# Score pairs of one map instead of two, and a value matmul in four parts, in a differential-attention encoder layer

## The reference

```python
s = jnp.einsum('bhqd,bhkd->bhqk', qblk, k, preferred_element_type=jnp.float32) * scale
p = jax.nn.softmax(s, axis=-1).reshape(B, N_HEADS, 2, Q_BLOCK, S)
a = p[:, :, 0] - lam * p[:, :, 1]  # differential attention map
return jnp.einsum('bhqk,bhkd->bhqd', a.astype(v.dtype), v)
```

## Time and profile before

| what | value |
|---|---|
| median of 3 runs (lowest, highest) | 4798.5 us (4790.17, 5101.57) |
| the profiled execution | 4784.27 us |
| its span on the slowest core | 4782.7 us (cores 4754.5 to 4782.7) |
| TensorE matmul busy | 4108.0 us (86%) |
| ScalarE busy | 2917.7 us (61%) |
| VectorE busy | 2577.9 us (54%) |
| GpSimd busy | 535.0 us (11%) |
| mean granted TensorE clock | 0.927 |
| moved by DMA | 752.94 MB, mean 157 GB/s |

### The profile page before, as it was taken

The page is one execution under the profiler, slowest core; times in us unless marked ns, Lnnn a source line. Parts: engine busy times, 40 slices in busy tenths (PEclk is TensorE's granted clock), DMA queues, the critical chain, the costliest instruction groups (busy, mean ns, idle before and its releaser), DMA issues.

```text
span 4782.7 us, 50532 instructions; the slowest of 8 cores (4754.5 to 4782.7 us)
## 1 busy us (share of the span) xinstructions
PE 4108.0 (86%) x18144; PEld 1551.1 (32%) x18144; DVE 2577.9 (54%) x4244; ACT 2917.7 (61%) x5274; POOL 535.0 (11%) x486
## 2 busy tenths in 40 slices
PE   6858666889898889896878898888899978999999
PEld 2312121223343333331223343323333323344344
DVE  2757545566434667675755425655677666323333
ACT  4658667778544668785877434567888866412411
POOL 1631010000001520000000003410000000000100
PEclk9978686999999999997989999999999989999999
DMA  9367796799895247779678752288777786524522
GB/s 231 82 156 154 168 190 135 166 187 195 182 253 169 82 124 155 141 165 200 130 162 204 196 142 73 68 201 206 174 158 167 150 206 153 183 84 154 187 87 80
DMA packets 1122593, 752.94 MB, mean 157 GB/s; under 512 B 917155, under 2 KB 1053606, under 8 KB 1097766
## 3 DMA queue, kind: packets, MB, share of 16 engines
q1 hardware_dynamic: 1044966, 507.47, 47.3%
q10 hardware_dynamic: 31968, 208.68, 13.4%
q0 software_dynamic: 45408, 33.56, 5.3%
HBM read 441.30 MB, written 115.34 MB: 116 GB/s over the span
## 4 chain that ended last, share of the span: by engine, by line
PE 46%; ACT 21%; DMA 15%; DVE 9%; issue 6%; POOL 2%; SPq 1%; ACTq 0%; DVEq 0%
PE pall L464 46%; ACT sb_ov L477 20%; DMA sb_ov<-sb_ov 13%; DVE sb_ov L488 5%; DVE sb_ov L485 3%; POOL sb_ov L485 2%; SPq L507 1%; ACT sb_sm L477 1%; DMA fr_d<-sb_ov 0%; DMA q_d<-sb_ov 0%; SPq L510 0%; DVE sb_sm L488 0%; DMA sb_ov<-x 0%; DVE sb_sm L797 0%; DMA sb_ov<-hT_d 0%
## 5 line engine op out<-in xcount | busy, mean ns | idle before, releaser
L464 PE MATMUL pall<-sb_ov 128*128 128x512 bf16 (+1 forms) x15588 | 3576.9, 392 | 521.2 <-ACT sb_ov L477 391.4
L477 ACT ACTIVATE sb_ov<-pall 128x1024 bf16<-128x1024 f32 (+2 forms) x2383 | 2036.9, 868 | 1207.4 <-PE pall L464 1002.0
L464 PEld LDWEIGHTS pall<-sb_ov 128*128 128x128 bf16 (+1 forms) x15588 | 1327.1, 98 | 2680.3 <-ACT sb_ov L477 723.2
L488 DVE SCALAR_TENSOR_TENSOR sb_ov<-sb_ov,sb_sm 128x2048 bf16<-128x2048 bf16 (+1 forms) x480 | 1026.3, 2138 | 255.4 <-ACT sb_sm L477 241.9
L485 DVE TENSOR_TENSOR sb_ov<-pall,sb_ov 128x512 f32<-128x512 f32 (+1 forms) x912 | 619.2, 690 | 600.4 <-PE pall L464 454.7
L485 POOL TENSOR_TENSOR sb_ov<-sb_ov 128x512 bf16<-128x512 f32 (+1 forms) x384 | 462.1, 1225 | 2334.9 <-DVE sb_ov L485 1837.7
L477 ACT ACTIVATE sb_ov<-sb_ov 128x512 f32<-128x512 f32 (+3 forms) x597 | 507.1, 850 | 239.6 <-DVE sb_ov L485 116.8
L485 DVE TENSOR_TENSOR sb_ov<-sb_ov 128x512 bf16<-128x512 bf16 (+2 forms) x530 | 348.1, 662 | 524.4 <-ACT sb_ov L477 465.2
L464 PE MATMUL pall<-sb_ov,sb_vall 128*128 128x512 bf16 x1536 | 398.8, 419 | 60.1 <-DMA sb_ov<-sb_ov 60.1
L477 ACT ACTIVATE sb_ov<-pall,sb_sm 128x512 f32<-128x512 f32 x384 | 262.5, 686 | 251.4 <-PE pall L464 115.0
L477 ACT ACTIVATION_READ_ACCUMULATOR sb_ov<-pall 128x1 f32 x1536 | 306.4, 199 | 0.0
(11 more groups left out here) (33 smaller groups left out, 223.9 us busy)
## 6 DMA issues: line engine op xcount, KB each, us to landing
sb_ov<-x SPq DMA_DIRECT2D x96, 512.0 KB, 8.0
sb_ov<-k_d SPq DMA_DIRECT2D x96, 512.0 KB, 4.8
sb_ov<-wb_g ACTq DMA_DIRECT2D x44, 1024.0 KB, 6.1
sb_ov<-wb_u ACTq DMA_DIRECT2D x40, 1024.0 KB, 5.6
sb_ov<-wb_d ACTq DMA_DIRECT2D x40, 1024.0 KB, 5.7
sb_ov<-wb_a ACTq DMA_DIRECT2D x44, 768.0 KB, 5.7
sb_ov<-hT_d SPq DMA_DIRECT2D x24, 1024.0 KB, 12.0
y<-sb_ov SPq DMA_DIRECT2D x48, 512.0 KB, 5.0
```

What stands on the lines that cost most here:

```text
L464: P.op("pe", lambda e: e.matmul(out, lhsT=lhsT, rhs=rhs, start=start, stop=stop), reads, writes, us)
L477: P.op("act", lambda e: e.activation(out=out, in_=in_, func=func, **kw), reads, writes, us)
L488: P.op(eng, lambda e: e.scalar_tensor_tensor(out=out, in0=in0, scalar=scalar, in1=in1, op0=op0, op1=op1), reads, writes, vus(eng, n) + 0.06)
```

## The change

A unit is now one map of one half: `sset(n, hh, m)` issues two score matmuls, key blocks 2hh and 2hh+1 of map m, one on rows 0 to 63 and one on rows 64 to 127, into the map's two banks, and one exponential. Before each unit stands a `Need` for its two banks alone. For that, k is stored with even key blocks on partitions 0 to 63 and odd ones on 64 to 127, both maps along the row, and q is stored twice, on both halves of the partitions. A q load is 256 KB into one of two buffers (three of 128 KB before); a q store is two DMAs. Buffers behind q move by 1 KB per partition. The value matmul yields an empty `Need` after 4, 8 and 12 of its 16 matmuls.

```diff
-    k_d = dscr("k_d", [8, 128, SEQ], BF16)
-    q_d = dscr("q_d", [8, 128, SEQ], BF16)
+    k_d = dscr("k_d", [8, 128, 2, 2, 512], BF16)
+    q_d = dscr("q_d", [8, 128, 2, SEQ], BF16)
...
-        A_T, A_K, A_Q, A_E1, A_E2, A_SQ, A_RS, A_D = 0, 32, 40, 43, 55, 63, 65, 69
+        A_T, A_K, A_Q, A_E1, A_E2, A_SQ, A_RS, A_D = 0, 32, 40, 44, 56, 64, 66, 70
...
-                    d, nm = (k_d, "k_d") if n < 32 else (q_d, "q_d")
-                    DMAL(d[hd % 8][:, c * 512:(c + 1) * 512], ovb(so, 512), ("st", n % 3), cells(so, 512), [(nm, hd % 8, c)], 128)
+                    if n < 32:
+                        dst = [(k_d[hd, 64 * (c % 2):64 * (c % 2) + 64, :, c // 2], ("k_d", hd, c))]
+                    else:
+                        dst = [(q_d[hd - 8, 64 * i:64 * i + 64, :, c * 512:(c + 1) * 512], ("q_d", hd - 8, c, i)) for i in range(2)]
+                    for i, (d, key) in enumerate(dst):
+                        DMAL(d.rearrange("d m t -> m d t"), ovb(so, 512), ("st", n % 3, i), cells(so, 512), [key], 128)
...
-                    for kc in range(2):
-                        for m in range(2):
-                            b = 2 * m + kc
-                            kk = klo_ + (2 * hh + kc) * 512
-                            MM(bank(b), ov[64 * m:64 * m + 64, qlo + qt * 128:qlo + (qt + 1) * 128],
-                               ov[64 * m:64 * m + 64, kk:kk + 512], True, True, cells(kk, 512) + cells(qlo, 512), [bk(b)], half=True)
+                    kk, q = klo[hi] + (2 * m + hh) * 512, (A_Q + 2 * (hi % 2)) * KB + m * 512 + qt * 128
+                    for i in range(2):
+                        MM(bank(2 * m + i), ov[64 * i:64 * i + 64, q:q + 128], ov[64 * i:64 * i + 64, kk:kk + 512], True, True,
+                           cells(kk, 512) + cells(q, 128), [bk(2 * m + i)], half=True)
...
-                        yield Need(keys=cells(klo[hi], 2048) + cells((A_Q + hi % 3) * KB, 512) + [bk(b) for b in range(4)])
-                        sset(n, 0)
+                        for m in range(2):
+                            yield Need(keys=cells(klo[hi], 2048) + cells((A_Q + 2 * (hi % 2)) * KB, 1024) + [bk(2 * m), bk(2 * m + 1)])
+                            sset(n, 0, m)
...
                     for kt in range(16):
+                        if kt and kt % 4 == 0:
+                            yield Need()
                         MM(bank(bo), vall[:, kt, h * 128:(h + 1) * 128], ovb(at + kt * 512, 512), kt == 0, kt == 15,
```

More of the change, by code:

```diff
@@ L730, in kload @@
                     lo = (A_K + 4 * i) * KB
-                    DMAL(ovb(lo, 2048), k_d[h], ("kl", i), [("k_d", h, c) for c in range(NTC)], cells(lo, 2048), 512)
+                    DMAL(ovb(lo, 2048).rearrange("p (m h t) -> p m h t", m=2, h=2), k_d[h], ("kl", i), [("k_d", h, c) for c in range(NTC)], cells(lo, 2048), 512)
                     return lo
                 def qload(c, h):
-                    lo = (A_Q + (c * 8 + h) % 3) * KB
-                    DMAL(ovb(lo, 512), q_d[h][:, c * 512:(c + 1) * 512], ("ql", (c * 8 + h) % 3), [("q_d", h, c)], cells(lo, 512), 128)
+                    i = (c * 8 + h) % 2
+                    lo = (A_Q + 2 * i) * KB
+                    DMAL(ovb(lo, 1024).rearrange("p (m t) -> p m t", m=2), q_d[h][:, :, c * 512:(c + 1) * 512], ("ql", i),
+                         [("q_d", h, c, x) for x in range(2)], cells(lo, 1024), 256)
                 for tau in range(67):
@@ L769, in xstream, with sset @@
                 NQ = len(hs) * 4
-                def sset(n, hh):
+                def sset(n, hh, m):
                     hi, qt = n // 4, n % 4
-                    klo_, qlo = klo[hi], (A_Q + hi % 3) * KB
-                    e1, e2 = E1[n % 3], E2[n % 2]
-                    for kc in range(2):
-                        for m in range(2):
-                            b = 2 * m + kc
-                            kk = klo_ + (2 * hh + kc) * 512
-                            MM(bank(b), ov[64 * m:64 * m + 64, qlo + qt * 128:qlo + (qt + 1) * 128],
-                               ov[64 * m:64 * m + 64, kk:kk + 512], True, True, cells(kk, 512) + cells(qlo, 512), [bk(b)], half=True)
-                    a = 16 + (n % 4) * 8
[L783 to L788, removed]
+                    kk, q = klo[hi] + (2 * m + hh) * 512, (A_Q + 2 * (hi % 2)) * KB + m * 512 + qt * 128
+                    for i in range(2):
+                        MM(bank(2 * m + i), ov[64 * i:64 * i + 64, q:q + 128], ov[64 * i:64 * i + 64, kk:kk + 512], True, True,
+                           cells(kk, 512) + cells(q, 128), [bk(2 * m + i)], half=True)
+                    a = 16 + (n % 4) * 8
+                    o = (E2[n % 2] if m else E1[n % 3]) + hh * 1024
+                    col = a + 2 * m + hh
+                    ACT(ovb(o, 1024).rearrange("p (a b) -> p a b", a=2), pall[:, 2 * m:2 * m + 2, :], AF.Exp,
+                        [bk(2 * m), bk(2 * m + 1)], cells(o, 1024) + [("acc", col)], 1024, scale=0.125,
+                        accum_out=sm[:, col:col + 1], ps=True)
                 def comb(n):
@@ L823, in xstream @@
                     if n < NQ:
-                        yield Need(keys=[bk(b) for b in range(4)])
-                        sset(n, 1)
+                        for m in range(2):
+                            yield Need(keys=[bk(2 * m), bk(2 * m + 1)])
+                            sset(n, 1, m)
                         if qt == 3 and hi + 2 < len(hs):
```

## The result

The kernel after takes 1.0459 of the time before, interval [1.0436, 1.0483]: slower by 4.6%, where 4745 us and "within 2%" were forecast. Some executions of every kernel here run longer, at a lower clock on some of the cores (this one's median over five runs, 5175.44 us, 5013.92 to 5319.07, holds such), and every ratio leaves them out. The profiled execution took 5014.25 us.

What follows compares the result with a forecast made beforehand. No engine is full in attention, where ScalarE and TensorE wait on each other; TensorE alone bounds the last stretch. Terms -54, -18, +8, +10 sum to -54: 4730 us, 4745 as median, own range 4700 to 4790 (8 in 10: 4620 to 4860).

Steps and rivals of the forecast that it cites:

- K and q layout: Storing q twice and loading 256 KB a head: taken as 0 us, upper end 31 us from 96 more issues.
- 1, lonely heads (-54): First sequence, heads with no MLP or gate matmuls beside them: 7.5 heads go from 26.2 to 19.0 us, -54 us.
- 2, stretches bound by loads (-18): Stretches where MLP and gate matmuls wait for their loads: attention gets 8.6 heads done instead of 6.3, -18 us.
- 3, filled heads (+8): About 54 heads with MLP or gate matmuls beside them: down -0.6, up +0.9 us each, together +8 us.
- Attention stages were to be shorter by 60 to 110 us each: Sign that the forecast is right: each of the three attention stages shortens by 60 to 110 us.
- The last stretch was to grow by 190: Sign that the forecast is right: the stretch after the last attention stage grows by some 190 us.
- 4, transposes (+10): Attention's transposes come denser, which can't make them land sooner: +10 us, range 0 to some 200.
- the slower rival: Transposes' landing becomes the bound in attention: 4930 us, chance 0.12; its sign is ScalarE waiting above 400 us for them.
- If units go singly, with a y group after each, the loop is gone and so is attention's lead: Rival: heads keep their place between groups of eight MLP or gate matmuls (y), time stays, 4800 us; chance 0.13.
- ScalarE's waits for TensorE would fall far below 1119 us: Sign that the forecast is right: ScalarE's total waits for TensorE fall far below the 1119 us of before.

Runs made afterwards that it cites:

- e8: Kernel before with only k's and q's store form changed (map as outermost dimension, each stored once, loads in two halves of 64 partitions): 1.0126 of before.
- e1: Kernel after with each k and q store cut into one per map (64 rows of 1 KB, same bytes): 0.9957 of before.
- e6: e3 with both maps' pairs of a half asked for together, value matmul still in one piece: 0.9938 of before.
- e5: e1 with both maps' pairs of a half asked for together on all four banks, value matmul in four parts: 0.9788 of before.
- e3: e1 with the value matmul in one piece again, pairs of one map still asked for singly: 1.0058 of before.

## Why the prediction was wrong

**The step that failed is "K and q layout".** It said that "the stores are in the projection, where no head waits for the queue", took 0 and gave 31 us as the upper end, from 96 more issues at 0.32 us. It counted issues at the duration of the old form, and looked for heads that wait. But the new store runs at 48 GB/s, as the kernel after and e8 show, and what waits is the projection's own chain, since only three store buffers stand between it and the queue. In its place stands: 32 q tiles a sequence, two stores of 2.7 us each against a tile every 2.6 us (first sequence), 2.8 us too much, 90 us a sequence (estimate); measured were 95, 56 and 75 for the projections as a whole, against 0 to 31 us for the whole run in the prediction. The trace of before had no row of the new form, and the nearest one (q's stores, 320 ns) was of the old form and gave no upper end. The rule by which it could have been told stands in the Trainium skill, in the section named above, and the prediction drew on another page instead. Without this step (e1) the kernel takes 0.9957, some 20 us less than before and not clear of no change, against a forecast of 54 less.

**1, lonely heads (-54).** The size of the head was nearly right: 19.0 forecast with ends of 18.0 and 20.5, 19.7 to 20.2 seen. The number of such heads was too high: five of the first sequence in the kernel before stood wholly without y, not 7.5 heads' worth. e6, where the pairs stand alone, has a first attention stage of 951 us: 23 less than before.

**2, stretches bound by loads (-18).** No run separates them.

**3, filled heads (+8).** Forecast were five y groups, ten changes of mode and 19.0 us; six, eleven and 21.4 to 21.8 came. The mode changes are the term that was too small: 54 heads with two more each are 22 us, while 318 more in the whole kernel are 64 by the same 0.2 us. With both maps asked for together (e5) the time is 81 us below e1's. The 21.4 to 21.8 are of good heads, as said above. The term's own sum is uneven, too: an up head's 21.0 holds half a microsecond for coupling, a down head's 19.0 a whole one; with one in both it would be some +20 instead of +8. Attention stages were to be shorter by 60 to 110 us each; they were by 33, 97 and 1. The last stretch was to grow by 190 and grew by 135: 668 y matmuls more behind the last scores at 0.202 us.

**4, transposes (+10).** ScalarE's wait for them went from 307 to 369 us, below the 400 given as the sign of the slower rival (412 and 407 in e3 and e6, beyond it). That rival isn't what made the kernel slower: attention got shorter.

**The rivals.** The slower one was looked for in the transposes' landing; the true one was a DMA, too, but a store. "If units go singly, with a y group after each, the loop is gone and so is attention's lead" was half right: they do go singly and it costs the pairs' gain, while the lead stays. That ScalarE's waits for TensorE would fall far below 1119 us was wrong as put (1167 in the kernel after, 1036 in e5), and the wrong thing to ask for: 391 of the 1119 us stand in the last stretch and 373 in attention, and in attention they did fall, to 236 (after) and 190 (e5).

## What to carry to other kernels

A store with the same bytes and the same run length can be several times slower when its outermost dimension is 2 instead of 128: read the pattern from the outside in, give 128 (or 64) rows first, and price it by a row of the same form or not at all. A cost hidden alone can surface when the same step is also doubled; multiply first, then compare with the time between two uses. And where a planner places the pieces, a finer unit is also one more place to be interrupted: count the mode changes for the whole kernel, and let units that belong together be asked for together (81 and 58 us here). Last, a wait summed over the whole run can stay the same while it moves from one stage to another: read it by stage.

## What the runs showed of the hardware that was not expected

With 128 rows outermost, nearly a whole store of 128 KB on SP's queue fell into one column of 0.575 us (219 to 226 GB/s over it). With the two maps outermost the same bytes took 2.7 us at 48 GB/s, with two or three packets on their way at once. As two stores of 64 rows (e1), SP took 597 ns to issue each, and in 31% of the stretch no packet was on its way; 64 KB in 597 ns are 110 GB/s, so the issues seem to set the pace there (estimate).

Where stores of the slow form are asked for faster than they are done, SP's issue of the next takes as long as a store (2632 ns in the kernel after); where one comes a tile, it takes 478 (e8), and 320 in the old form (before). A pair of changes between whole-array and row-tiled matmuls costs 0.19 us in the starts of the matmuls (before).
